# Where the operands of the matmuls lie in SBUF: weights at 64 past a multiple of 128 bytes, activations on one

## What is computed

```python
z = h @ w_in
merged = (gates[:, :, 0] * (y_na @ w_br_na) + gates[:, :, 1] * (y_mla @ w_br_mla)
          + gates[:, :, 2] * (y_gqa @ w_br_gqa))
return merged @ w_out
...
return (jax.nn.gelu(g) * a) @ w_down
```

## The kernel before

| buffers | use | place modulo 128 |
|---|---|---|
| `wraw`, `whi`, `wlo` | weights, their high and low parts | 0 |
| `H` (high and low parts side by side) | input of most products | 32 |
| `y0` | first branch's output, then the high part of the merged one | 0 |
| `cqn`, `ckn` | normed latents | 96 |
| `y1`, `y2` | other branches' outputs (`y1` then the low part of the merged one) | 96 |
| `fh`, `fl`, `gh`, `gl`, `ym`, `ydh`, `ydl` | hidden layers, RWKV's and the dilated layer's outputs | 0 |

## Time and profile before

### The profile page before, as it was taken

One profiled execution on the slowest core, in us unless ns is written; L12 is line 12 of the kernel. 1 busy time (PEld: TensorE's weight loads), 2 busy tenths in 40 slices (PEclk: granted clock), 3 DMA queues, 4 the chain that ended last, 5 costly groups with the idle time before them and its releaser, 6 DMA issues. The chain is left out here.

```text
span 1599.8 us, 28596 instructions
## 1 busy us (share of the span) xinstructions
PE 1571.2 (98%) x11814; PEld 1421.1 (89%) x11814; DVE 1093.3 (68%) x1702; ACT 947.5 (59%) x1563; POOL 295.2 (18%) x214
## 2 busy tenths in 40 slices
PE   9999999999999999999999999989999999999998
PEld 7999998999899999989998897768888899878886
DVE  5775656887457665568864677678944678789744
ACT  6777756665457877566654665346533666665531
POOL 0000210443000002104420143016500021118300
PEclk9999999999999999999999999999999999999999
DMA  8343454565553434545555531225565435345651
GB/s 330 120 154 137 150 194 183 193 231 183 189 185 105 172 119 149 215 152 200 195 186 183 225 117 71 75 95 203 208 217 204 189 132 185 106 184 186 237 197 65
DMA packets 42321, 272.77 MB, mean 170 GB/s; under 512 B 4816, under 2 KB 4944, under 8 KB 13392
## 3 DMA queue, kind: packets, MB, share of 16 engines
q1 hardware_dynamic: 41184, 265.18, 46.7%
q10 hardware_dynamic: 1008, 5.77, 1.0%
HBM read 269.88 MB, written 1.05 MB: 169 GB/s over the span
## 5 line engine op out<-in xcount | busy, mean ns | idle before, releaser
L317 DVE TENSOR_TENSOR b_wlo<-b_wraw,b_whi 128x2048 fp32r<-128x2048 f32 (+3 forms) x261 | 565.2, 2169 | 180.2 <-PE b_ps L471 124.9
L309 ACT ACTIVATE b_whi<-b_wraw 128x2048 fp32r<-128x2048 f32 (+3 forms) x262 | 466.3, 1781 | 200.1 <-PE b_ps L471 148.3
L390 PE MATMUL b_ps<-b_H,b_whi 128*128 128x256 f32 x1704 | 483.2, 284 | 0.2
L393 PE MATMUL b_ps<-b_H,b_wlo 128*128 128x256 f32 x1704 | 476.3, 280 | 0.0
L392 PE MATMUL b_ps<-b_H,b_whi 128*128 128x256 f32 x1704 | 476.2, 279 | 0.0
L390 PEld LDWEIGHTS b_ps<-b_H,b_whi 128*128 128x128 f32 x1704 | 321.0, 188 | 8.3 <-issue 6.8
L392 PEld LDWEIGHTS b_ps<-b_H,b_whi 128*128 128x128 f32 x1704 | 321.1, 188 | 0.6
L393 PEld LDWEIGHTS b_ps<-b_H,b_wlo 128*128 128x128 f32 x1704 | 320.9, 188 | 0.0
L436 PE MATMUL b_ps<-b_H,b_whi 128*128 128x512 f32 x448 | 155.7, 391 | 0.0
L1597 POOL TENSOR_TENSOR b_fl<-b_ab,b_fh 128x256 fp32r<-128x256 f32 x44 | 93.6, 2128 | 213.4 <-ACT b_fh L1570 213.4
L437 PE MATMUL b_ps<-b_H,b_wlo 128*128 128x256 f32 x448 | 126.3, 282 | 0.0
(11 more groups left out here) (367 smaller groups left out, 2721.9 us busy)
## 6 DMA issues: line engine op xcount, KB each, us to landing
b_wraw<-in_w SPq DMA_DIRECT2D x221, 1024.0 KB, 4.8
b_wraw<-in_w SPq DMA_DIRECT2D x35, 512.0 KB, 3.6
b_wraw<-in_w SPq DMA_DIRECT2D x6, 768.0 KB, 6.0
b_bias<-in_rpb SPq DMA_DIRECT2D x8, 512.0 KB, 6.5
b_gains<-in_gains ACTq DMA_DIRECT2D x4, 1024.0 KB, 4.9
b_X<-in_x ACTq DMA_DIRECT2D x2, 512.0 KB, 5.4
b_cA<-in_cA SPq DMA_DIRECT2D x2, 512.0 KB, 6.1
out<-b_X SPq DMA_DIRECT2D x4, 256.0 KB, 2.1
```

The source lines that it names most:

```text
L309: e.activation(whi[u % NHI][:, 0:n], raw[u % NRAW][:, 0:n], ACT.Copy).then_inc(up("w_hi", "whi", u))
L317: e.tensor_tensor(wlo[u % NLO][:, 0:n], raw[u % NRAW][:, 0:n], hi.bitcast(F32), ALU.subtract).then_inc(up("w_lo", "wlo", u))
L390: e.matmul(out, wh, x.hi[:, kk, :], start=k == 0, stop=False)
L393: ins = e.matmul(out, wl, x.hi[:, kk, :], start=False, stop=last)
```

## The change

It moves buffers and nothing else. A function `place` takes up the bytes to the next address with a given remainder modulo 128. The seven buffers `whi` and `wlo` now begin 64 bytes past a multiple of 128; `H` comes ahead of `X` and `c1` and begins on a multiple of 128, as do `cqn`, `ckn`, `y1` and `y2`. The calls ahead of `y0`, `fh`, `gh`, `ym` and `ydh` find these already on a multiple. `wraw` does not move. Of buffers that no float32r matmul reads, those behind `ckn` in the mixer (queries, keys and values of two attentions, the bias, `mg`) go from 96 to 0 as well. Every engine's instructions, their order and their waits are the same as before.

```diff
+    def place(ctx, offset=0):
+        n = (offset - nc.sbuf_base) % 128
+        if n:
+            sb(ctx, "gap", [P, n // 4])
+
     raw = ring(top, "wraw", NRAW, [P, UNIT])
+    place(top, 64)
     whi = ring(top, "whi", NHI, [P, UNIT], F32R)
     wlo = ring(top, "wlo", NLO, [P, UNIT], F32R)
+    place(top)
+    H2 = sb(top, "H", [P, 8, 2, T], F32R)
     X = sb(top, "X", [P, 2, D])
     c1 = sb(top, "c1", [P, sum(w for _, w in at1.values())])
-    H2 = sb(top, "H", [P, 8, 2, T], F32R)
...
+                place(s1)
                 self.y0 = sb(s1, "y0", [P, 8, T], F32R)
...
+                place(s1)
                 cqn = [sb(s1, "cqn", [P, 3, T], F32R) for _ in range(2)]
                 ckn = [sb(s1, "ckn", [P, 2, T], F32R) for _ in range(2)]
...
+                    place(s2)
                     self.y1, self.y2 = sb(s2, "y1", [P, 8, T], F32R), sb(s2, "y2", [P, 8, T], F32R)
...
+                place(s1)
                 fh, fl = sb(s1, "fh", [P, 22, T], F32R), sb(s1, "fl", [P, 22, T], F32R)
...
+                place(s1)
                 fh, fl = sb(s1, "gh", [P, 32, T], F32R), sb(s1, "gl", [P, 32, T], F32R)
...
+                place(s1)
                 self.ym = sb(s1, "ym", [P, 8, T], F32R)
...
+                place(s1)
                 yh, yl = sb(s1, "ydh", [P, 8, T], F32R), sb(s1, "ydl", [P, 8, T], F32R)
```

## The result

The changed kernel takes 1613.72 us (median of 6 runs, 1613.56 to 1616.71), the kernel before on the same chip 1600.59 us (6 runs, 1599.22 to 1602.81). The ratio is 1.0086, its 95% interval 1.0073 to 1.0099: 13 us slower, where 30 us faster was forecast. It lies inside the range of 1538 to 1619, but only because that range reached into rival 4 for a slower kernel, to which I had given 0.25; the forecast's own 1550 to 1590 missed.

The account below looks back on a forecast made before the run. TensorE bounds the kernel by how fast one matmul starts after another. Half of a 67 us upper bound, 33 us gained, less 3 lost as waits, gives 1570 us; own range 1550 to 1590, 8-in-10 range 1538 to 1619.

Parts of the forecast that it names:

- rival 4: Slower: tile form on `H` goes from 116.7 to 120.0 ns, losing 16.9 us; 1618 us, or 1627; chance 0.25.
- The split of the weights: L309 and L317, writing and reading at 64 instead of 0: put at nothing, any per cent or two hidden under TensorE.
- The signs named for being wrong: Tile form staying at or above 116.7 ns, or distances falling as said while the span doesn't.
- The term of rival 4 for the aligned row form: Row form on `gh` and `fh` going from 226.7 to 233.3 ns: 1296 x 6.6 = 8.6 us on top.
- the two streams: Moving operand and next matmul's stationary one, meeting in SBUF: read as the excess of 10.0 to 13.3 ns per matmul.
- about 111.7 ns at 256 columns and 216 at 512: What float32r matmuls could reach if the streams didn't meet, taken from two fp32 groups.
- the upper bound: Gain if the streams no longer met: 60.9 us, 67 with small groups; 13.9 of it from row form on `gh`, `fh`.
- I take the half: Streams assumed to meet half as much at 64 apart: 33 us gained; no row tells the fraction.
- no row has two operands 64 apart: Claim that the profile shows no matmul with the pair of places which the change makes everywhere.
- The 4 us that the row form on `H` was to give back: Within rival 4: the row form on `H` and `y` gives 4 us back.
- the point from which it decides: Tile form's distance above 117.5 ns while the aligned row form stays makes the kernel slower; 4.4 us / 5688 = 0.8 ns.
- The tenth of a gain that was to return as a wait: In the mixers and at the norms, where other engines carry the chain: 3 us of the gain lost again.

Follow-up runs that it names:

- experiment 10: Changed kernel with `fh`, `gh`, `ydh` put at distance 0 from the weights: 1606.80 us, ratio 1.0029 to the kernel before.
- experiment 2: Measuring-only kernel: eight pairs of places, weight loads of 128, 64 and 32 columns, each in float32r and fp32; 650.68 us.
- experiment 5: Measuring-only kernel: tile, wide and row forms with activations 0 to 480 bytes past the weights, weights beginning at 0, 64 and 128; 422.16 us.
- experiment 6: Changed kernel with places set modulo 256, weights at 192, every activation at 128: 1598.66 us, ratio 0.9996 to the kernel before.
- experiment 11: Changed kernel with `fh`, `gh`, `ydh` 128 bytes from the weights modulo 256: 1611.89 us, ratio 1.0066 to the kernel before.
- experiment 9: As experiment 6, but row-form inputs `fh`, `gh`, `ydh` at distance 0 from the weights: 1588.28 us, ratio 0.9933 to the kernel before.
- experiment 1: Measuring-only kernel: float32r matmuls of 256 and 512 columns at each pair of operand places modulo 128, in steps of 16 bytes; 372.08 us.
- the twelve beginnings: Measuring-only kernel: 48 tile-form matmuls at each of five distances after a wait or various row-form, fp32 or float32r matmuls; 386.06 us.

## Why the prediction was wrong

**Right.** TensorE sets the end, by the distance between its starts; that distance depends on the places of the operands, by a few per cent; and count times distance accounts for the change (13.9 us for 12.0). The split of the weights, put at nothing, cost nothing, and the busy totals of VectorE, ScalarE and GpSimd moved by 1.8 us at most (947.5 to 949.3 for ScalarE); the single writers weren't looked at. The signs named for being wrong did their work: the tile form stood at 117.5 ns, above 116.7. The term of rival 4 for the aligned row form, 226.7 to 233.3 for 1296 matmuls, was 8.6 us; 8.5 were measured, and experiment 10 gives them back alone.

**Wrong, the step that failed: "I read it as the two streams ... meeting in SBUF while both run", with its floors of "about 111.7 ns at 256 columns and 216 at 512".** The whole forecast of 33 us rested on it. A load of a quarter of the columns leaves the excess at 512 columns (experiment 2), so it isn't a cost that lasts as long as the load does. That the time depends on the distance between the moving and the stationary operand does speak for the two reads bearing on each other; how is not shown, and every matmul in every run has its load, so no run tells what is left without one. And fp32, from which I took the floors, shows no effect of place at all, so it couldn't show what float32r does when nothing meets. The lowest that any place gave with loads of 128 columns is 113.3 ns for 256 columns and 226.6 for 512: 6.6 and 13.3 ns over, a sixteenth of the columns and not a fixed 3 to 5 ns. At 512 columns the kernel before already stood at this floor in its aligned row form. There was nothing to gain in the 1296 matmuls to which I gave 13.9 us of the upper bound, only the 6.6 ns each to lose. "I take the half" halved a number that had no ground.

**Wrong: the period.** I showed that 64 isn't a period and then worked modulo 128, the modulus of the change, without testing it. It is 256 (experiments 5, 6, 11). The change puts the activations 64 past the weights; the tile form's good distance is 192. So "no row has two operands 64 apart" was true, but what 64 is depends on which side: at 64 the tile form has 117.8, at 192 113.3. Had I added up addresses modulo 256, the kernel's rows would have shown distances 32, 0 and 224, and no reason to hold 64 better.

**Rival 4 had the sign and not the sizes.** Its main term, the tile form going to 120.0 for 16.9 us, came out as 117.7 for 2.6 to 4.0. What it named second, the row form, was the greater part. The wide form, "perhaps 3", lost 2.8. The 4 us that the row form on `H` was to give back did not come: it stayed at 233.3, since 32 and 64 cost it the same (experiment 5). Nor did the point from which it decides hold as put: 117.5 ns in the tile form was reached just as it says, but with the row form moved as well, and it left out the wide form's 3 us. The tenth of a gain that was to return as a wait found no gain to apply to; in experiment 9 it would have been 1.7 us and was 0.2.

**The Trainium skill, weighed again.** It says that TensorE has two independent SBUF read ports (TensorE: Matmul & The Clock Gate, part 2, the step on LDWEIGHTS). What I concluded from it, that the place could then not matter, is contradicted: 113.3 to 120.0 ns for one shape at one clock, with no other engine at work (experiments 1 and 5). The gap that the same part of the Trainium skill gives for a single matmul, columns over 2.4 GHz plus about 2.5 ns, fits fp32 at its two cycles a column (512 columns: 2 x 512 / 2.4 = 426.7, and 429.2 for each of the two shown) and no float32r row here.

**Open.** Why the period is 256 and what the sixteenth of the columns is. Why the address counts in steps of 16 bytes. Which rhythm a stretch falls into: the twelve beginnings show no rule, and it is not even shown that the beginning decides. What the wide form does at distance 64. And the wide form is best at 32 and the tile form at 192, both on `H`; a version with two copies or with the wide form's stages at another place was not tried.

## What to carry to other kernels

Where TensorE is the bound with float32r, the place of one operand relative to the other, modulo 256 bytes, was worth up to 6% of a matmul and 0.7% of this kernel; fix that distance for each form by itself (tile 192, row 0, wide 32 here, all at multiples of 32) and not one alignment for all. Before moving buffers, spend one small kernel on the map of distances, and one control that shifts everything; a few rows of the kernel in hand don't tell the period, nor the floor. Trace more than one execution where a stretch can run in two rhythms: one alone credits an edit with what may be chance. A floor is taken from the same data type at its best place, not from another type that happens to be near.

## What the runs showed of the hardware

- Float32r matmuls of 256 columns, each with a load of 128, follow each other every 113.3 to 120.4 ns in nearly all places (one of 123.3), those of 512 columns every 226.6 to 236.8, at the full granted clock (experiment 1); the best are a sixteenth over the columns. Fp32 ones take 431.7 and 858.4 ns at every place tried (experiment 2).
- For operands at multiples of 32 bytes the time depends on the distance of the two modulo 256, and a shift of all by 64 bytes leaves it (ratio 1.0004); it does so differently for each form: 192 is best in the tile form, worst but one in the wide form. In steps of 16 bytes the address counts too: 226.7 and 233 to 234 ns in turn at one distance (experiment 1).
- A stretch without waits can run in one of two steady rhythms (117.8 or 113.3 ns at distances 192 and 64) and keeps it for a whole feed-forward, some 100 us (experiments 6, 9 and 11). What picks it isn't shown.
